# Gated delta rule on one core: moving the product with the inverse and the subtraction within a tile

## What is computed

```python
a_mat = jnp.where(strict, bc[..., :, None] * jnp.einsum('...id,...jd->...ij', kc, kc) * decay, 0.0)
tinv = lax.linalg.triangular_solve(eye + a_mat, jnp.broadcast_to(eye, a_mat.shape), left_side=True, lower=True)
value = tinv @ (vc * bc[..., None])
kcum = tinv @ (kc * (bc * jnp.exp(gam))[..., None])
def step(s, xs):
    val, kcm, qkm, qd, kd, gl = xs
    u = val - kcm @ s
    o = qd @ s + qkm @ u
    s = s * gl + jnp.swapaxes(kd, -1, -2) @ u
    return s, o
```

## Time and profile before

| what | value |
|---|---|
| median of 3 runs (lowest, highest) | 2233.78 us (2228.09, 2234.16) |
| the profiled execution's own time | 2229.45 us |
| its span, first to last instruction | 2227.8 us |
| mean granted clock of PE | 0.988 |
| PE busy | 2144.7 us, 96% |
| DVE, ACT, POOL busy | 1023.6, 573.0, 1110.3 us |

### The profile page before, as it was taken

How to read it: one execution, slowest core, us unless ns; L and a number is a source line. 1 busy time by engine, 2 the same in 40 slices (tenths; PEclk the granted TensorE clock), 3 DMA queues, 4 the chain that set the end, 5 groups by cost and what they waited for, 6 DMA issues and landing times. The chain is left out here.

```text
span 2227.8 us, 32773 instructions
## 1 busy us (share of the span) xinstructions
PE 2144.7 (96%) x12394; PEld 1585.3 (71%) x12394; DVE 1023.6 (46%) x1937; ACT 573.0 (26%) x1252; POOL 1110.3 (50%) x1063
## 2 busy tenths in 40 slices
PE   9998999899999999989999999999999999999997
PEld 6775555476777777767776667677767777777776
DVE  5433676436331233068698655555541354213412
ACT  2103677501000000036565343443410100000011
POOL 2322555257564465276576452534355476535652
PEclk9999899999999999999999999999999999999999
DMA  8536201911212221252222333232232222122221
GB/s 275 155 100 220 97 1 53 329 67 68 76 57 76 95 76 58 83 178 78 64 70 77 108 95 99 95 113 89 88 119 76 76 76 76 76 76 76 76 76 43
DMA packets 125911, 216.45 MB, mean 97 GB/s; under 512 B 73602, under 2 KB 96002, under 8 KB 109762
## 3 DMA queue, kind: packets, MB, share of 16 engines
q1 hardware_dynamic: 119234, 197.13, 26.4%
q0 software_dynamic: 3088, 14.03, 1.7%
q10 hardware_dynamic: 3440, 3.25, 0.4%
HBM read 185.08 MB, written 37.55 MB: 100 GB/s over the span
## 5 line engine op out<-in xcount | busy, mean ns | idle before, releaser
L2015 PE MATMUL ps<-xn,ring 128*128 128x288 f32 x768 | 198.8, 407 | 5.4 <-DVE xn L2118 3.2
L2015 PE MATMUL ps<-hid,ring 128*128 128x288 f32 x768 | 192.9, 406 | 0.0
L2015 PEld LDWEIGHTS ps<-xn,ring 128*128 128x128 f32 x768 | 145.3, 190 | 48.3 <-DVE xn L2118 5.9
L2015 PEld LDWEIGHTS ps<-hid,ring 128*128 128x128 f32 x768 | 145.6, 190 | 40.8 <-ACT p L2052 0.9
L2052 ACT ACTIVATE p<-ps 128x288 f32<-128x288 f32 x48 | 19.7, 411 | 597.3 <-PE ps L2015 597.3
L2098 POOL TENSOR_TENSOR prod<-prod,rstd 128x1152 f32<-128x1152 f32 x32 | 83.9, 2622 | 178.7 <-DVE prod L2182 162.4
L3741 PE MATMUL ps<-xn,ring 128*128 128x288 f32 x512 | 146.2, 420 | 4.0 <-PE ps L3849 1.9
L2015 PE MATMUL ps<-x_sum,wsum 128*128 128x288 f32 x512 | 130.6, 407 | 3.4 <-DVE x_sum L2122 1.9
L1123 POOL TENSOR_SCALAR ring<-ring,fac 128x128 f32<-128x128 f32 (+2 forms) x96 | 92.5, 980 | 82.7 <-DVE fac L1552 82.7
L2072 POOL TENSOR_TENSOR wsum<-ring 128x512 f32<-128x512 f32 x64 | 82.0, 1282 | 99.2 <-DMA ring<-in_w_mlp 91.3
L2015 PE MATMUL ps<-hid_sum,wsum 128*128 128x288 f32 x512 | 128.4, 407 | 0.1
(11 more groups left out here) (602 smaller groups left out, 4576.2 us busy)
## 6 DMA issues: line engine op xcount, KB each, us to landing
ring<-in_w_mlp SPq DMA_DIRECT2D x64, 1024.0 KB, 4.8
ring<-in_w_gdn_in SPq DMA_DIRECT2D x16, 1024.0 KB, 4.9
ring<-in_w_nsa_in SPq DMA_DIRECT2D x9, 1024.0 KB, 5.5
ring<-in_w_gdn_z SPq DMA_DIRECT2D x8, 1024.0 KB, 5.0
x<-in_seq_state SPq DMA_DIRECT2D x4, 2048.0 KB, 12.2
out_seq_state<-x SPq DMA_DIRECT2D x4, 2048.0 KB, 6.6
ring<-in_w_gdn_out SPq DMA_DIRECT2D x8, 1024.0 KB, 4.9
out_win_old<-in_win_rows POOLq DMA_DIRECT2D x1, 8064.0 KB, 44.6
```

The source lines that it names most:

```text
L2015: mm = nc.tensor.matmul(S.ps[:, base + BANK[p], 0:HT], stationary(p, blk.units[pair // 4], pair % 4), moving(blk.kind, p, pair), start=pai ...
```

## The change

On PE, the tile's steps and the next tile's join steps are interleaved in another order: both halves of the queries' product ahead of join step 1, the product with the inverse between join steps 1 and 2, the new state ahead of step 3; the output product is issued as two halves of two heads, one ahead of join step 4 and one behind the turn. The pauses of tile 0 stand one step later. On DVE, `rest` (the subtraction) comes ahead of the mask of join step 1, and the addition of step 2 behind `new_values`. The reciprocal of chunk 14 goes from the tiles of hg 1 to the samples' section of hg 0. In attention, `sample_news` and `sample_normal` each go one place later.

```diff
--- before.py
+++ after.py
@@ -1672,9 +1672,9 @@
                         cmp_normal(step // 2)
                     if (step, s) == (0, 1):
                         sample_center()
-                    elif (step, s) == (0, 2):
+                    elif (step, s) == (0, 3):
                         sample_news()
-                    elif (step, s) == (0, 3):
+                    elif (step, s) == (1, 0):
                         sample_normal()
                     elif (step, s) == (1, 3):
                         sample_out()
@@ -3638,6 +3638,8 @@
                 for j in range(4):
                     mm = nc.tensor.matmul(bank_at(w.b, 1)[:, col(j)], B["qk"][:, j, :], B["u"][:, j, :], start=w.i == 0, stop=True,
                                           skip_group_check=True)
+                    if j == 1:
+                        yield
                 done(mm, c, "pe")
                 yield
 
@@ -3782,11 +3784,8 @@
                     if 0 < i < 3:
                         keys_turned(tile(hg, i + 1))
                     next(used)
-                    next(joins, None)
                     next(used)
                     next(joins, None)
-                    if i == 0:
-                        pause(2, 2)
                     next(used)
                     next(joins, None)
                     if i == 0:
@@ -3794,6 +3793,10 @@
                     if i == 3:
                         seq_products(hg)
                         fill(1)
+                    next(used)
+                    next(joins, None)
+                    if i == 0:
+                        pause(2, 2)
                     next(used)
                     next(joins, None)
                     if last:
@@ -4172,16 +4175,16 @@
                     pass
                 if hg == 0:
                     unit_length(13)
-                late = unit_pieces(15 - hg) if hg < 2 else iter(())
+                late = unit_pieces(15) if hg == 0 else iter(())
                 for i in range(PT):
                     last = norm_before(hg, i) if i else None
                     norm = norm_sum(*last) if last else iter(())
                     joins = join(w[i + 1]) if i and w[i + 1] else iter(())
                     next(norm, None)
-                    next(joins, None)
                     rest(w[i])
                     next(joins, None)
                     new_values(w[i])
+                    next(joins, None)
                     next(joins, None)
                     next(norm, None)
                     new_state(w[i])
@@ -4202,10 +4205,16 @@
                 dve.wait_ge(zm_zero, 1)
                 wait_step(dve, Q, "pool", hg, "qdec")
                 qd = wide[0]["qdec"]
+                last_unit = unit_pieces(14) if hg == 0 else iter(())
                 for j in range(4):
+                    if j == 2:
+                        next(last_unit, None)
+                        next(last_unit, None)
                     dve.wait_ge(zm_used, hg * 4 + j + 1)
                     v.tensor_copy(bass.AP(S.shared, ZM_AT + 512 * (j % 2) + 256, [[SHARED, 128], [128, 2], [32 + TD, 4], [1, TD]]),
                                   qd[:, TS * j:TS * j + TS].rearrange("p (a n t) -> p a n t", a=2, t=TD)).then_inc(zm_q, 1)
+                next(last_unit, None)
+                next(last_unit, None)
                 wait_step(dve, Q, "pe", hg, "value")
                 done(v.tensor_tensor(B["u"][0:TS], S.ps[0:TS, 1, :].rearrange("p (j v) -> p j v", j=4),
                                      S.beta[0:TS, PT, 4 * hg:4 * hg + 4].unsqueeze(2).broadcast_to([TS, 4, 128]), ALU.mult), Q, "vec")
```

## The result

The changed kernel takes 2245.36 us (median of 11 runs, 2237.87 to 2249.83), the kernel before 2231.66 us beside it: a ratio of 1.0063, 95% interval 1.0053 to 1.0074, so 12 to 16.5 us slower. The profiled execution took 2244.36 us, its span is 2242.7 us and the mean granted clock 0.986. Between the first transposition of the delta rule (L3527) and the first matmul behind it (L2290) lie 440.15 us where there were 427.29: 12.86 of the 14.91 us between the two profiled executions are in this stage.

What follows compares the result with a forecast made beforehand. PE's waits, released by DVE's queue and ACT's copies, were taken to decide. Head groups +7.84, tile 0 +0.4, hg 1 -2.81 or -1.4, attention +0.75: +6.2 or +7.6; 2229.45 + 6.9 + 2.2 = 2238.5 us, range 2230 to 2247.

Steps and rivals of the forecast that it cites:

- the likeliest case: Whole kernel: the sum as worked out, +6.2 us, or +7.6 with a low-clock stretch left; chance 45%.
- more of the tiles run at the lower clock: Rival, delta rule's tiles: three to five low-clock tiles instead of one, 1.4 us each, 2242 to 2245 us; chance 25%.
- hg 1's gain: Tiles 1 and 2 of hg 1 without chunk 14's reciprocals: 2.81 us saved, or 1.4 if a low-clock stretch stays.
- the signs named: Profile after: tiles 1 and 2 of hg 2 and hg 3 about 2 us longer, those of hg 1 about 1 shorter.
- The 6.7 us that a measurement was said to need: Whole kernel: about 0.3%, 6.7 us, is what a measurement can tell from no change.
- The wait ahead of the inverse's product: Tiles 1 and 2: PE idle about 1.3 us ahead of L3626, released by DVE's subtraction.
- The shift of 0.98 us a tile: Tiles 1 and 2 of each head group: the turn starts 0.98 us later, delaying the next tile as much.
- Step 5: Join step behind the turn: PE idles some 0.7 us ahead of it instead of 0.18, waiting for ACT's copies.
- The half that covers the mask of step 4: Output product's first half, 0.55 us, ahead of join step 4: pays for itself by covering DVE's mask.
- Reciprocals hidden in hg 0: Chunk 14's reciprocal pieces fit into DVE's waits of 3.79 and 2.87 us in hg 0's samples' section, costing nothing.
- The attention's +0.75: Attention: the samples' turn on PE starts 0.75 us later, with bounds of -1.2 and +1.0 us.
- Tile 0's pauses: Tile 0 of each head group: the product starts 0.1 us later than the first pause did, 0.4 us for four.

Runs made afterwards that it cites:

- e10_sub_first_alone: The changed kernel with DVE's subtraction ahead of the norm's sum and scaling, and the attention's samples where they stood before: 2232.49 us, 1.0012.

## Why the prediction was right, and where it fell short

The direction was right and 2245 lies in the range; the number was 6.9 us too low, half of the rise, because the likeliest case was not the one that came. What came is the rival "more of the tiles run at the lower clock": four stretches, inside "three to five", at 1.40 us measured against 1.4 taken, and a time just above its 2242 to 2245. That the time fits so well is partly luck: the rival's sum lacked the scaling's 1.2 us and had shifts of 0.98 us where about 1.1 came, and against that hg 1's gain was 2.3 us and not 1.4. Of the signs named, hg 2 and hg 3 came out 3.70 and 4.02 us longer instead of about 2, and hg 1 0.79 us longer instead of 1 shorter. The 6.7 us that a measurement was said to need were too many: the interval is some 2.3 us wide on either side.

*The wait ahead of the inverse's product* (1.3 us): right in hg 1 to 3 where the scaling is short, 1.15 to 1.33 us. In hg 0 it is 1.51 and 2.50 us, since a reciprocal piece of 1.34 us stands ahead of the sum there; the prediction saw that the shift would stay the same, and did not ask what the piece does to the wait. *The shift of 0.98 us a tile*: nearly right, 1.1 to 1.2. Taking the change of the scaling and 1.4 us for a new low-clock stretch from the periods leaves 1.10 and 1.20 (hg 0), 1.22 and 1.10 (hg 2), 1.09 and 1.11 (hg 3). *Step 5*: 0.62 us against 0.7. *The half that covers the mask of step 4*: right, by the run with the product whole. *Reciprocals hidden in hg 0*: right (DVE still waits 0.35 us ahead of the new values when they alone are moved, though the 1.4 us wait in the prediction's bound stands in no row); with 1.1 us of shift taken off, both tiles of hg 1 are 1.1 to 1.2 us shorter, and the move alone saves 2.9 us.

*The attention's +0.75*: the samples' turn starts 18.59 us behind L1141 where it was 17.87, 0.72 later, on PE:

```profile
220.59 1.89 PE L1167 MATMUL ps<-qkv 64*128 64x256 f32 x4 [1.81 <-ACT ring L1383]
224.33 1.92 PE L1250 MATMUL ps<-cst,xn 128*31 128x128 f32 x8 [1.85 <-DVEq L1627]
```

Whether it reaches the end stays open: 0.2 to 4.5 us in one comparison, no difference to be seen in the other.

*Tile 0's pauses* (0.1 us each) is one of the two steps that failed. On PE it holds: from tile 3 of the head group before to tile 1 the time grew by 0.00 us (hg 2) and 0.06 (hg 3). But the z product's last piece stands in the second of these pauses, and SP's queue waits for it with the ring's load (L3326), behind which the load of the grown queries (L3322) is issued. Timeline of SP's queue, hg 2, before (first row) and after:

```profile
1459.86 0.33 SPq L3326 DMA_DIRECT2D ring<-in_w_gdn_z  x1
1466.68 0.33 SPq L3326 DMA_DIRECT2D ring<-in_w_gdn_z  x1
1467.06 0.44 SPq L3322 DMA_DIRECT2D gdn_tiles<-gate_rows_scratch  x1
```

The ring's load starts 1469.47 - 1466.68 = 2.79 us ahead of tile 1's L3604; in the kernel before, 1459.86 stands 3.65 us ahead of 1463.51. POOL's growth of the queries comes later against the tile by this 0.86 us, and falls on DVE's scaling.
The sum of the tiles: eight shifts of 1.1 (8.8), scalings 1.2, three more stretches of 1.4 (4.2), hg 1's reciprocals -2.3: +11.9, against 12.1 measured in the periods. Of the 0.7 us more in the stage, 0.15 lie ahead of hg 0's tile 1 and 0.53 between hg 0's tile 3 and hg 1's tile 1. There the samples' scaling, beside POOL too, takes 1.93 us where it took 1.53; in the runs in which it takes 0.25 to 0.26 us, that piece is 74.64 to 74.77 us long instead of 75.18 before and 75.71 after. In the profiled executions the stage also starts 0.87 us later, and 1.2 us more are lost behind it, where nothing was changed.

Most of the loss (11 of 14 us) comes of one line of DVE's order: with the sum and the scaling still ahead of the subtraction, the wait that the new order was to fill becomes longer. With the line moved, PE's waits filled and the attention as before, the new order reaches 2229.70 us, no better than the old order with the reciprocals moved. That one (2227.92) and the one with the late scaling (2227.51) are the only two whose intervals lie below the kernel before.

## What to carry to other kernels

When a PE product is moved ahead of work that used to cover its operand's delay, move its producer's queue neighbours too: look at what stands between the last input and the producer on that engine, and not on PE alone. A step that is moved takes its signals along: follow each of them through the DMA queue to the engine behind it, since a small operation that was free can fall into the shadow of a large one. Where TensorE's waits grow beyond those that the trace shows at full clock, price the lower clock with them, as a chance and not as a certainty, and try filling the wait before giving the order up.

## What had not been expected of the hardware

A DVE scaling of 128 x 4 numbers takes 0.16 to 0.17 us alone and up to 1.42 us in tiles 1 and 2 beside POOL's operations, ending 0.03 us after one of them in the places shown; the sums (0.63 to 0.69 us) and the subtractions (1.02 to 1.13) keep their times in every run. Not every operation of POOL does it: inside its L3137 (0.85 us) the scaling took 0.17 us in `e10_sub_first_alone`. And the executions of one and the same kernel go with the clock: the 12 runs with the subtraction first take 2229.37 and 2230.85 us at a mean granted clock of 0.989, and 2239.80 us at 0.983. And the clock need not fall at the same places: two runs with the same wait of 1.52 us differ in it. A single profiled execution is thus one draw of how often the clock falls: that of the run with the attention as before was its fastest (2227.87 us, median 2232.49), and its stage length hid the cost that the median showed.
